# A chunked delta-rule layer on TensorE: the turns of the triangular inverse, as full transposes and as 64 by 64 products

## The reference

```python
kb = k * beta[..., None]
a = jnp.where(strict, jnp.einsum('bhncd,bhnsd->bhncs', kb, k) * decay, 0.0)
lower = a + jnp.eye(CHUNK, dtype=f32)
u = lax.linalg.triangular_solve(lower, v * beta[..., None], left_side=True,
                                lower=True, unit_diagonal=True)
w = lax.linalg.triangular_solve(lower, kb * jnp.exp(gc)[..., None], left_side=True,
                                lower=True, unit_diagonal=True)
```

## Time and profile before

| | |
|---|---|
| median of 3 runs | 2388.55 us (2388.48 to 2388.66) |
| the profiled execution's own time | 2389.01 us |
| its span, first to last instruction | 2387.5 us |
| TensorE (PE) busy | 2352.2 us, 99% |
| PEld busy | 1940.8 us, 81% |
| VectorE (DVE) busy | 1444.7 us, 61% |
| ScalarE (ACT) busy | 959.2 us, 40% |
| GpSimd (POOL) busy | 159.9 us, 7% |
| granted TensorE clock, mean | 0.999 of full speed |

### The profile page before, as it was taken

One profiled execution on the slowest core, in us unless ns is written; L12 is line 12 of the kernel. 1 busy time (PEld: TensorE's weight loads), 2 busy tenths in 40 slices (PEclk: granted clock), 3 DMA queues, 4 the chain that ended last, 5 costly groups with the idle time before them and its releaser, 6 DMA issues.

```text
span 2387.5 us, 36244 instructions
## 1 busy us (share of the span) xinstructions
PE 2352.2 (99%) x12558; PEld 1940.8 (81%) x12558; DVE 1444.7 (61%) x2121; ACT 959.2 (40%) x1714; POOL 159.9 (7%) x167
## 2 busy tenths in 40 slices
PE   6999999999999999999999999999999999999998
PEld 4888888888888888888888888888888888888886
DVE  7797662454778665255568866525457885642644
ACT  4576321223466532122346643212234764321232
POOL 0121000000012000000001200000000120000000
PEclk9999999999999999999999999999999999999999
DMA  4222223233322223223332122222433213222241
GB/s 155 101 72 72 93 96 103 89 138 117 125 80 72 81 89 98 97 95 136 119 125 72 62 95 91 97 97 97 141 120 120 71 46 106 97 97 97 97 146 66
DMA packets 64003, 236.60 MB, mean 99 GB/s; under 512 B 7568, under 2 KB 7696, under 8 KB 62720
## 3 DMA queue, kind: packets, MB, share of 16 engines
q1 hardware_dynamic: 55728, 201.98, 25.0%
q0 software_dynamic: 8144, 32.94, 3.9%
HBM read 226.47 MB, written 8.42 MB: 98 GB/s over the span
## 4 chain that ended last, share of the span: by engine, by line
PE 87%; DVE 8%; issue 2%; ACT 2%; DMA 0%; DVEq 0%; ACTq 0%; POOL 0%; POOLq 0%
PE ps L1443 86%; DVE w_l L859 1%; PE ps L1601 1%; PE ps L1662 1%; DVE nq L986 1%; DVE nq_l L991 0%; DVE h_l L1377 0%; DVE qkvz L1048 0%; DVE acc L873 0%; DVE qkvz L1052 0%; DVE ti L1273 0%; DVE sm L1023 0%; DVE state L1259 0%; DVE qk L1040 0%; DVE at L1021 0%
## 5 line engine op out<-in xcount | busy, mean ns | idle before, releaser
L1443 PE MATMUL ps<-h_h,w_h 128*128 128x512 f32 x2004 | 792.9, 396 | 8.8 <-DVE h_l L884 4.6
L1443 PE MATMUL ps<-h_l,w_h 128*128 128x512 f32 x2004 | 782.7, 391 | 0.0
L1443 PE MATMUL ps<-h_h,w_l 128*128 128x512 f32 x1972 | 768.1, 390 | 0.0
L477 ACT CAST w_h<-stage 128x1024 fp32r<-128x1024 f32 x381 | 398.3, 1045 | 559.5 <-PE ps L1443 559.4
L859 DVE TENSOR_TENSOR w_l<-stage,w_h 128x1024 fp32r<-128x1024 f32 x381 | 466.7, 1225 | 251.5 <-ACT w_h L477 238.0
L1443 PEld LDWEIGHTS ps<-h_h,w_h 128*128 128x128 f32 x2004 | 377.3, 188 | 107.5 <-DVE h_l L884 10.8
L1443 PEld LDWEIGHTS ps<-h_l,w_h 128*128 128x128 f32 x2004 | 377.8, 189 | 77.0 <-issue 1.9
L1443 PEld LDWEIGHTS ps<-h_h,w_l 128*128 128x128 f32 x1972 | 370.4, 188 | 77.9
L1443 PE MATMUL ps<-ff_h,w_h 128*128 128x512 f32 x1036 | 404.6, 391 | 0.0
L1443 PE MATMUL ps<-ff_l,w_h 128*128 128x512 f32 x1036 | 403.1, 389 | 0.0
L1443 PE MATMUL ps<-ff_h,w_l 128*128 128x512 f32 x1036 | 403.1, 389 | 0.0
(11 more groups left out here) (192 smaller groups left out, 1872.3 us busy)
## 6 DMA issues: line engine op xcount, KB each, us to landing
stage<-w SPq DMA_DIRECT2D x385, 512.0 KB, 3.3
x_next<-x POOLq DMA_DIRECT2D x20, 512.0 KB, 6.1
out<-xs POOLq DMA_DIRECT2D x32, 256.0 KB, 2.2
rowb<-row_copy POOLq DMA_DIRECT2D x4, 1024.0 KB, 5.0
xs<-x POOLq DMA_DIRECT2D x8, 512.0 KB, 4.8
xs<-x POOLq DMA_DIRECT2D x4, 1024.0 KB, 5.4
bia<-bias POOLq DMA_DIRECT2D x1, 1024.0 KB, 6.3
cst<-con POOLq DMA_DIRECT2D x2, 192.0 KB, 3.2
```

Source lines behind the costliest of these rows:

```text
L477: act.copy(w_h[:, b, 0:k], stage[:, s, 0:k]).then_inc(w_hi.sem, 1)
L1443: return pe.matmul(o, a, b, start=start, stop=stop)
```

## The change

On PE `turn` is no longer a transpose. For each head and each diagonal 64x64 block the block of `ti` is the stationary operand of an ordinary product with a 64x64 identity: 8 products a tile in the place of 4 transposes. The block at rows and columns 0 to 63 and the one at 64 to 127 use different quadrants of the array, and write partitions 0 to 63 and 64 to 127 of the same 256 columns of bank `lev(t)`. A no-operation now stands ahead of each tile's products. On ACT `flip` copies only these two blocks per head into `xi`, as two instructions of 64 partitions and 4x64 elements, in place of one of 128x512. Everything outside the blocks stays zero from POOL's memset. What is waited for and signalled does not change.

```diff
@@ ACT, flip
                     act.wait_ge(p_x.sem, p_x.after(g, l * TILES + t + 1))
-                    act.copy(xi[:, t], heads(lev(t))).then_inc(x_ready.sem, 1)
+                    for e in range(2):
+                        r = chunk(e)
+                        last = act.copy(xi[r, t, :, r], ps[r, lev(t), 0:HEADS * HD].rearrange("p (h c) -> p h c", h=HEADS))
+                    last.then_inc(x_ready.sem, 1)
@@ PE, turn
                     pe.wait_ge(t_ready.sem, t_ready.after(g, l * TILES + t + 1))
-                    four(heads(lev(t)), lambda o, h: pe.transpose(o, ti[:, t, h], I), p_x)
+                    pe.nop(nofuse=True)
+                    for h in range(HEADS):
+                        for e in range(2):
+                            r = chunk(e)
+                            last = mm(ps[r, lev(t), HD * h:HD * h + HD], ti[r, t, h, r], cst[r, K_ID, r])
+                    last.then_inc(p_x.sem, 1)
```

## The result

The change takes **2392.78 us** (median of 20 runs, 2391.49 to 2394.01) where the kernel before, on the same chip, takes 2388.91 (20 runs, 2387.77 to 2390.22). The ratio is 1.0015 with a 95% interval of 1.0009 to 1.0021: slower by 3.9 us, where 0.4 to 0.8 was forecast (against 2388.91, the forecast's 2389.3 would be +0.4; its working has +0.8). The median lies outside the range.

What follows compares the result with a forecast made beforehand. TensorE, busy for 99% of the span, was taken to bound the kernel. Per group -0.10 +0.25 +0.05 = +0.20 us, 0.8 over four, gave 2389.8 from the profiled execution, 2389.3 us by the median; 8-in-10 range 2388.0 to 2391.6.

Steps and rivals of the forecast that it cites:

- Part 1: TensorE's products for transposes: 0.058 to 0.060 us a pair; per group first turns save 0.07 to 0.14, second cost 0.23 to 0.29.
- Rival A: On TensorE the two diagonal blocks take turns, pair period up to 0.120 us: 2404 us, slower by 0.66%; chance 8%.
- Part 2: TensorE's added no-operation per tile: hidden except at the fourth tile of the first turns, 0 to 0.08 us, taken 0.05.
- rival C: On TensorE the no-operations show at all 32 tiles, 0.05 us each: +1.6 us, 2390.9; chance 5%.
- Part 3: ACT's 64 smaller copies, spaced 0.27 us, 0.54 a tile, covered by 0.4 us before `masked(1,3)`: cost nothing.
- Rival B: ACT's copies don't overlap and hold `masked`: 0.3 us a group, perhaps as much in the second stage, +1.2 to +2.4; chance 9%.
- The sum: Whole kernel, per group: -0.10 +0.25 +0.05 = +0.20 us, 0.8 us over four groups.

Runs made afterwards that it cites:

- e2: The change with its products, but ACT makes one 128x512 copy a tile, reading the 256 columns twice (output wrong, for time only): 2389.59 us, ratio 1.0004.
- e6: The change with the loop over blocks outside that over heads, so a tile's first-block products precede its second-block ones: 2395.18 us, ratio 1.0028 to the kernel before.
- e4: The change with copies grouped by block: for two tiles at a time both low blocks, then both high ones: 2394.2 us, ratio 1.0024 to the kernel before.
- e1: The kernel before, full transposes kept, with only the change's copies (two of 64x256 a tile, one per partition half): 2392.33 us, ratio 1.0015.
- e7: The change with the order of the two copies reversed in every odd tile: 2390.57 us, ratio 1.0008 to the kernel before.
- e3: The kernel before, each tile's copy split by heads into two of 128x256 on all partitions: 2388.74 us, ratio 1.0001.
- e5: The kernel before with the change's products in the first stage only, copied there as one 128x256 per tile; second stage as before: 2388.0 us, ratio 0.9998.

## Why the prediction was wrong

- **Part 1, the products: right, term by term.** First turns -0.09 a group (forecast -0.07 to -0.14), second turns +0.26 to +0.27 (+0.23 to +0.29), a pair 0.059 to 0.060 us. e2 gives the part alone.
- **Rival A, the blocks take turns: refuted.** 0.059 per pair is far from 0.120. The Trainium skill's rule (TensorEngine Tiling (Array Packing), Restrictions and Gotchas) does not bind these blocks, which lie in different row halves and write different partitions of one bank; the measurement decides. That the two blocks do share the time is shown by e6, where changing their order alone adds 0.77 us a group.
- **Part 2 and rival C, the no-operations:** the first stage came out at -0.09 in total, inside what part 1 gives without them. The 0.05 at the fourth tile wasn't needed; e2 has the same -0.09. No gap at any tile bound.
- **Part 3, the copies: this step failed.** "L723 has that shape: 370 ns, two together in 0.64 us, so spaced 0.27" took the spacing from a row whose two copies are on the same partitions. The change's copies alternate between partitions 0 to 63 and 64 to 127. A tile takes 0.77 us (0.38 and 0.39), not 0.54; the chosen value lay at the wrong end of the bounds 0.54 to 0.74, and even the upper bound was a little low. So the 0.4 us of cover at the fourth tile was a shortfall, and a cost put at nothing measured 0.60 us a group in `masked(1)`. The exponentials behind the second stage's copies slipped by 1.05 us, not by 0.4 (they start 184.05-182.25 = 1.80 us behind `ov(1)`, before 183.14-182.39 = 0.75), and that cost another 0.10.
- **Rival B was the mechanism, and its price too small.** Its copy rows are right: fourth tile at 172.55+3.05 = 175.60 (it had 175.5). Its price of 0.3 a group measured 0.60. It left out the step from ACT's end to TensorE's start, which is 0.14 in the change (above) and 0.15 in e4 (the third copy, which makes the first tile ready, ends at 173.03+1.01 = 174.04, and `masked(1)` starts at 174.19), it had 0.1 us too few for the copies, and `masked(1)` wants the tile 0.04 to 0.05 earlier since the turns save 0.09. Its "as much in the second stage" didn't come: `masked(2)` never waited, but the exponentials came later, +0.10 at `ov(2)` (0.22 in e1). What spoke for B, the four separate pieces, wasn't the reason either: e4 and e7 have the same pieces.
- **The sum.** Forecast +0.2 a group; measured +0.88 = +0.18 from the products (as forecast) +0.70 from the copies. One group has +0.25 more from a gap. The chance of 9% and the upper end of B, +2.4, came from treating "the same shape" as "the same case", and pricing a wait without the semaphore step behind it.

## What to carry to other kernels

Before a copy is split into two by partitions, ask whether the engine will still overlap them, and take the spacing from a row in which the partitions change as they will; the mean duration of one said nothing about it here (416 ns overlapped, 367 did not). A merged row gives that in one division, its length less one duration over the count less one. Where cover is a few tenths of a us, price the bad bound with all its steps, the step from engine to engine too. If the split can't be avoided, reverse the order in every other tile: here that alone gave back 2 of 3.9 us.

## What the runs showed of the hardware

**ACT copies overlap by partitions.** Start to start, with 256 elements per partition in fp32: 0.27 us where the next copy is on the same partitions (64 partitions in e4 and e7, all 128 in e3), 0.38 to 0.39 where it goes from one half to the other. All eight copies in a stage of e1, the change, e4, e6 and e7 fit these numbers. The PSUM bank isn't what decides: in the change the two copies of a tile read one bank and the next tile's read another, and neither step overlaps, while e3's copies overlap within a bank and e4's between two. Nor is a start at partition 64: e4 and e7 overlap there too. Why the change of partitions matters isn't shown.

**Quadrants overlap past a neighbour.** e6's 0.039 us a record, between 0.030 for alternating blocks and 0.060 for one quadrant.

**Single gaps in dense stretches of small products.** In the second group of the change `update(1)` takes 0.25 us longer. The row of the change, then that of the kernel before:

```profile
764.79 2.31 PE L1446 MATMUL ps<-dl,xi 64*64 64x32 f32 x64
```

```profile
764.59 2.06 PE L1443 MATMUL ps<-dl,xi 64*64 64x32 f32 x64
```

No semaphore stands there. Such gaps, 0.1 to 0.6 us, appear in five of the six kernels with the products (the change, e2, e4, e5, e7), once or twice in each, in `update(1)` or in the first turns, and not in before, e1 and e3. Each ends 1.3 to 1.5 us after the landing of a packet on the queue of instructions, of which the change has 78 in place of 74 (the page's line of that queue):

```profile
q8 instruction: 78, 1.28, 0.2%
```

The products leave four times the records of the transposes they replace, so TensorE may run up against the fetching of its own instructions. That is argued from the timing, not tried, and against it stands that most such packets bring no gap (16 land in the four stretches of the change, for one gap), and that e5 has two gaps with the 74 packets of before. The gap accounts for 0.25 us of the 3.9.
